# First product for V placed in column block 30 of peer_u, and the routing done by halves of the tokens and of the heads

## The chip, the cores and the metric

The kernel runs on one core of one Trainium2 chip. The metric is the device time of one execution in microseconds (us). The core has five engines, each with its own stream of instructions, in order: TensorE (PE: matmuls, and PEld for loading their stationary operand), VectorE (DVE), ScalarE (ACT), GpSimd (POOL) and SyncE (SP, which here only issues DMAs). They wait for one another through semaphores. DMA queues move data between device memory (HBM) and the on-chip memory (SBUF); matmuls write into 8 banks of PSUM.

## The reference

Two transformer blocks on 256 tokens of width 2048, all in float32. The change concerns the expert layer (PEER) of the first block. With 128 x 128 = 16384 experts, each token picks 16 experts for each of 8 heads by its scores against two sets of 128 sub-keys; the result is a sum over those experts:

```python
s = einsum('thpd,hpnd->thpn', q, sub_keys)          # token, head, half p, key n
s_half, i_half = top_k(s, 16)
cand = s_half[:, :, 0, :, None] + s_half[:, :, 1, None, :]       # 16 x 16 sums
top_s, pos = top_k(cand, 16)
idx = take_along_axis(cand_idx, pos)                # cand_idx = i0 * 128 + i1
g = softmax(top_s)
a = einsum('cd,ced->ce', x, expert_u[idx])
y = einsum('ce,ced->cd', g * gelu(a), expert_v[idx])
```

## The kernel before

**Dense instead of gathered.** The kernel doesn't gather rows of expert_u and expert_v. It multiplies all tokens with all of peer_u, takes gelu of all 256 x 16384 products, multiplies them with a matrix of gates that is zero except where a token picked an expert, and multiplies the result with all of peer_v. The gates lie in a scratch tensor in HBM, scr_g (16384 experts x 256 tokens), which is cleared earlier. The gelus lie in scr_a.

**Pieces.** Weights come in pieces of 128 x 1024 (512 KB). For each piece, in a fixed order, SyncE loads `raw` (NR = 5 buffers), ScalarE rounds it to `whi` (L1512), VectorE forms the rest `wlo` = raw - whi (L1746), and TensorE makes three products, whi and wlo with the high part and whi with the low part of the activations (L1322). whi and wlo have NH = 3 buffers each, so VectorE can be at most about two pieces ahead of TensorE. peer_u takes 256 pieces in 32 column blocks j of 8 pieces each; peer_v takes 256 pieces, 16 groups `sc` of 16. After each column block of peer_u, ScalarE takes gelu, TensorE transposes it, and SyncE stores it to scr_a (L2303).

**Routing.** It runs beside peer_u. For each half t of the tokens (128 of 256): 16 selections of the best 16 of 128 (`top16`, five instructions each, L1987 to L1995), the casts and sums of candidates (L2000, L2006), 8 selections of 16 of 256, the softmax (`gate_gap` L2013, `gate_exp` on ScalarE, `gate_norm` L2020 to L2024), the way back from places to keys (`rank_halves`, `rank_match`, `rank_pick`, `rank_sum`, L2032 to L2055) and `expert_ids` (L2061 to L2065).

**Scatters.** For every head and rank GpSimd issues one indirect DMA (`gate_scatter`, L2252) that adds 128 gates, one per token, to scr_g: 16 for a head, 128 for a half of the tokens, 256 in all. The first scatter of a head waits until the last of the head before it, of the same tokens, has landed. Behind the last one `fetch(sc)` brings the gelus (L2261) and the gates (L2262) of one group of experts back on chip. `prepare(sc)` multiplies the two on VectorE (`expert_gate`, L2079) and splits the product into its high part (ScalarE) and low part (`expert_split`, L2086). It consists of four parts with two products each, and peer_v's group sc reads it. `fetch` of group sc + 2 follows prepare(sc).

**What sets the order.** The program writes out all engines' instructions in one walk. Generators in two lists, `tasks` and `idle`, are advanced at each `step()`; the first of `idle` one step with (nearly) every piece. The routing is in `idle`, the scatters are in `tasks`, four per step. The walk knows nothing of time: "the scatters are done" means only that they are all written into GpSimd's stream. So with four scatters in a step, the program has written all 256 long before GpSimd can have run them. In the kernel before, the routing generator ends with both first fetches and `prepare(0)`, four steps after that.

Of the kernel before, what the change touches and what calls it, by code (L numbers as in the profile page):

```python
# [38 lines left out]
def build(nc, D, out):  # L39
# [12 lines left out]
    with ExitStack() as ctx:  # L52
# [134 lines left out]
        def walk(steps):  # L187
# [694 lines left out]
            def scatter():  # L882
                landed, rounds, t = [t_clear, t_clear], [0, 0], 1
                while len(g_written) < 2:
                    while not routed:
                        yield
                    if len(routed) == 2 and rounds[1 - t] < 8:
                        t = 1 - t
                    elif len(routed) == 1:
                        t = 0  # L890
                        if rounds[0] == 8:
                            yield
                            continue
                    h = rounds[t]
# [6 lines left out]
                    rounds[t] += 1  # L901
                    if rounds[t] == 8:
                        g_written.append(mark)

            def routing():
                tasks.append(scatter())
                for t in range(2):
                    for hp in range(16):
                        go("top16", SC[:, t, hp, :], V16[:, t, hp, :], I16u[:, t, hp, :], fresh("DVE", t_sc, everything))
                        last = up("DVE", "top16")  # L910
                        yield
                    go("i16_cast", t, fresh("DVE", last))
                    last = up("DVE", "i16_cast")
                    for h in range(8):
                        if h == 4:
                            yield
                        go("candidates", t, h, fresh("DVE", last))
                        last = up("DVE", "candidates")
                    yield
                    for h in range(8):  # L920
                        go("top16", cand[:, h].rearrange("p a b -> p (a b)"), W2[:, h, :], P2u[:, h, :], fresh("DVE", last))
                        last = up("DVE", "top16")
                        yield
                    sm, ri = stat(8), stat(8)
                    go("gate_gap", fresh("DVE", last))
                    a = up("DVE", "gate_gap")
                    go("gate_exp", fresh("ACT", a))
                    a = up("ACT", "gate_exp")
                    go("gate_norm", t, sm, ri, fresh("DVE", a))
                    tg = up("DVE", "gate_norm")  # L930
                    yield
                    go("rank_halves", fresh("DVE", last))
                    a = up("DVE", "rank_halves")
                    for q in range(2):
                        for h in (0, 4):
                            hs = slice(h, h + 4)
# [9 lines left out]
                    go("expert_ids", t, fresh("DVE", a))  # L946
                    routed.append([tg, up("DVE", "expert_ids")])
                    yield
                while len(g_written) < 2:
                    yield  # L950
                bar.append(everyone())
                fetch(0)
                fetch(1)
                for _ in range(4):
                    yield
                yield from prepare(0)
# [59 lines left out]
            for j in range(32):  # L1016
                pair, b, last = gemm("peer_u", 8 * j, 16, AH, AL, nA)
                u_post(pair, b, last, j)
                if j == 0:
# [3 lines left out]
                    idle.append(routing())  # L1023
            while len(wB.get(0, ())) < 4:
# [475 lines left out]
        def scalar_program(e):  # L1500
# [122 lines left out]
            def gate_exp(ready):  # L1623
# [811 lines left out]
```

## Time and profile before

| what | us |
|---|---|
| median of 3 timed runs | 3737.26 (3732.13 to 3737.8) |
| the profiled execution | 3733.21 |
| its span, first to last instruction | 3731.4 |
| TensorE busy | 3291.7 (88% of the span) |
| VectorE busy | 2052.6 (55%) |
| ScalarE busy | 1489.1 (40%) |
| GpSimd busy | 502.2 (13%) |

The profiler's page divides the span into 40 equal slices of 93 us and gives each engine's busy tenths, the granted TensorE clock in tenths of full speed, and the mean busy share of the DMA engines:

```profile
PE   7888999999000699999999999999999999999998
DVE  7666549874000344566666666555446555555556
POOL 2110000578777200000000000000000000000000
PEclk9989999999555899999999999999999999999999
DMA  4336556788222666677777765655465656666664
```

A time is read from the span's start. All views in this document come from this one execution. PE's busy time is modelled for pipelined matmuls, and an instruction's idle time is put down to the engine whose semaphore came last. The spans of GpSimd's instructions that issue a DMA show the issuing, not the transfer.

### The profile page before, as it was taken

What the parts mean: (1) busy time and instruction counts of PE and PEld (TensorE: products, weight loads), DVE (VectorE), ACT (ScalarE), POOL (GpSimd) and SP (SyncE); (2) the same over time, 40 slices, a digit from 0 to 9 for tenths busy, and PEclk for the clock granted to TensorE, in tenths of its full rate; (3) what the DMA queues carried; (4) which work ended last, traced back from release to release, by engine and by line L of the source; (5) the groups of instructions that cost most, each with busy time, mean ns of one, the idle gap of its engine ahead of it and who ended that gap; (6) DMA issues with size and microseconds to landing.
All of it is one profiled execution on the core that took longest, in us unless ns stands there. A gap on an engine that the chain in (4) does not pass through costs nothing.

```text
span 3731.4 us, 44636 instructions
## 1 busy us (share of the span) xinstructions
PE 3291.7 (88%) x18254; PEld 2867.0 (77%) x18254; DVE 2052.6 (55%) x2880; ACT 1489.1 (40%) x1883; POOL 502.2 (13%) x332
## 2 busy tenths in 40 slices
PE   7888999999000699999999999999999999999998
PEld 6667897878000588888888887898999799999996
DVE  7666549874000344566666666555446555555556
ACT  3345444444000344444444445444444454444443
POOL 2110000578777200000000000000000000000000
PEclk9989999999555899999999999999999999999999
DMA  4336556788222666677777765655465656666664
GB/s 156 114 110 229 170 176 198 207 203 209 12 0 0 197 209 208 200 245 248 249 239 239 237 193 167 186 152 164 147 181 181 197 159 189 188 187 187 186 191 152
DMA packets 214941, 659.07 MB, mean 177 GB/s; under 512 B 56097, under 2 KB 56097, under 8 KB 212177
## 3 DMA queue, kind: packets, MB, share of 16 engines
q1 hardware_dynamic: 165536, 598.74, 51.6%
q0 software_dynamic: 49200, 57.49, 7.4%
q8 instruction: 144, 2.36, 0.3%
q14 instruction: 61, 0.49, 0.0%
HBM read 620.35 MB, written 35.78 MB: 176 GB/s over the span
## 4 chain that ended last, share of the span: by engine, by line
PE 68%; POOL 11%; issue 4%; DVE 4%; DMA 2%; ACT 1%; DVEq 0%; ACTq 0%; POOLq 0%
PE bank L1322 67%; POOL scr_g L2252 11%; DMA scr_g<-M 2%; DVE wlo L1746 1%; PE bank L1364 1%; ACT whi L1512 0%; ACT M L1502 0%; DMA M<-scr_g 0%; DVE TMP L1809 0%; DVE R L2180 0%; DVE TMP L1810 0%; DVE M L1989 0%; ACT M L1554 0%; DVE M L1995 0%; DVE AL L1786 0%
## 5 line engine op out<-in xcount | busy, mean ns | idle before, releaser
L1746 DVE TENSOR_TENSOR wlo<-raw,whi 128x1024 fp32r<-128x1024 f32 x1101 | 1352.3, 1231 | 1126.0 <-ACT whi L1512 1121.8
L1512 ACT ACTIVATE whi<-raw 128x1024 fp32r<-128x1024 f32 x1101 | 1161.0, 1059 | 1371.0 <-PE bank L1322 1344.4
L1322 PE MATMUL bank<-whi,AH 128*128 128x512 f32 x1664 | 664.3, 399 | 319.0 <-DVE wlo L1746 318.8
L1322 PE MATMUL bank<-whi,AL 128*128 128x512 f32 x1664 | 653.1, 392 | 0.0
L1322 PE MATMUL bank<-wlo,AH 128*128 128x512 f32 x1664 | 652.6, 392 | 0.0
L1322 PE MATMUL bank<-whi,BH 128*128 128x512 f32 (+1 forms) x1608 | 626.1, 389 | 0.1
L1322 PE MATMUL bank<-wlo,BH 128*128 128x512 f32 (+1 forms) x1608 | 623.5, 388 | 0.0
L1322 PE MATMUL bank<-whi,BL 128*128 128x512 f32 (+1 forms) x1608 | 623.0, 387 | 0.0
L1322 PEld LDWEIGHTS bank<-whi,AH 128*128 128x128 f32 x1664 | 315.6, 190 | 387.6 <-DVE wlo L1746 316.8
L1322 PE MATMUL bank<-AH,whi 128*128 128x256 f32 (+1 forms) x2064 | 591.3, 286 | 0.3
L1322 PE MATMUL bank<-AH,wlo 128*128 128x256 f32 (+1 forms) x2064 | 583.9, 283 | 0.0
L1322 PE MATMUL bank<-AL,whi 128*128 128x256 f32 (+1 forms) x2064 | 583.8, 283 | 0.0
L2252 POOL DMA_INDIRECT scr_g<-M x256 | 430.8, 1683 | 479.0 <-issue 444.4
L1322 PEld LDWEIGHTS bank<-AH,whi 128*128 128x128 f32 (+1 forms) x2064 | 395.2, 191 | 2.1 <-DVE AL L1786 1.1
L1322 PEld LDWEIGHTS bank<-AL,whi 128*128 128x128 f32 (+1 forms) x2064 | 395.2, 191 | 0.9
L1322 PEld LDWEIGHTS bank<-AH,wlo 128*128 128x128 f32 (+1 forms) x2064 | 394.9, 191 | 0.1
L1322 PEld LDWEIGHTS bank<-whi,AL 128*128 128x128 f32 x1664 | 314.9, 189 | 68.0
L1322 PEld LDWEIGHTS bank<-wlo,AH 128*128 128x128 f32 x1664 | 315.7, 190 | 62.5
L1322 PEld LDWEIGHTS bank<-whi,BH 128*128 128x128 f32 x1608 | 302.7, 188 | 67.4 <-DVE wlo L1746 6.4
L1322 PEld LDWEIGHTS bank<-whi,BL 128*128 128x128 f32 x1608 | 302.8, 188 | 62.1
L1322 PEld LDWEIGHTS bank<-wlo,BH 128*128 128x128 f32 x1608 | 302.9, 188 | 60.6
L1502 ACT ACTIVATE BH<-M 128x512 fp32r<-128x512 f32 x96 | 60.2, 632 | 457.9 <-DVE M L2079 457.2
(238 smaller groups left out, 2012.4 us busy)
## 6 DMA issues: line engine op xcount, KB each, us to landing
raw<-in_peer_u SPq DMA_DIRECT2D x256, 512.0 KB
raw<-in_peer_v SPq DMA_DIRECT2D x256, 512.0 KB
raw<-in_w_in SPq DMA_DIRECT2D x160, 512.0 KB
raw<-in_w_up SPq DMA_DIRECT2D x128, 512.0 KB
raw<-in_w_down SPq DMA_DIRECT2D x128, 512.0 KB
raw<-in_w_out SPq DMA_DIRECT2D x64, 512.0 KB
raw<-in_w_in_a SPq DMA_DIRECT2D x32, 512.0 KB
scr_g<-M POOLq DMA_DIRECT2D x8, 2048.0 KB, 24.7
```

Source lines behind the costliest of these rows:

```text
L1322: return e.matmul(outp, l, r, start=start, stop=stop)
L1364: last = e.transpose(banks[bank][:, 128 * n:128 * n + 128], s, ident)
L1502: e.activation(o, x, func, **kw).then_inc(sem(name), 1)
L1512: e.activation(whi[:, n % NH, :], raw[:, n % NR, :], ACT.Copy).then_inc(s_hi, 1)
L1746: e.tensor_tensor(wlo[:, n % NH, :], raw[:, n % NR, :], bf(whi[:, n % NH, :]), ALU.subtract).then_inc(s_lo, 1)
L2252: e.indirect_dma_start(out=D["scr_g"].rearrange("e (t o) -> (e t) o", o=1), out_offset=bass.IndirectOffsetOnAxis(ap=EID[t][:, k:k + 1], ax ...
```

## The change

Three things are changed. The routing of each half of the tokens is done for heads 0 to 3 and then for heads 4 to 7, so that expert ids are ready in four portions instead of two; each portion's scatters may be issued as soon as it is ready. `gate_norm` stands behind the rank steps instead of ahead of them. And the first two fetches are written at column block j = 28 of peer_u, the first product `prepare(0)` after block 30, instead of right behind the routing. The step functions get the slice `hs` of four heads (expert_ids is shown, the others likewise); their instructions are the same on half as many columns. The line numbers of the kernel after are up to 2 higher or lower.

```diff
@@ -880,60 +880,57 @@
             def scatter():
-                landed, rounds, t = [t_clear, t_clear], [0, 0], 1
+                landed, rounds, n, t = [t_clear, t_clear], [[], []], 0, 1
                 while len(g_written) < 2:
-                    while not routed:
+                    while routed:
+                        half, ready = routed.pop(0)
+                        h0 = 4 * (n % 2)
+                        n += 1
+                        rounds[half] += [(h, ready) for h in range(h0, h0 + 4)]
+                    if rounds[1 - t]:
+                        t = 1 - t
+                    elif not rounds[t]:
                         yield
...
-                        go("gate_scatter", t, 16 * h + k, fresh("POOL", routed[t], landed[t] if k == 0 else None))
+                        go("gate_scatter", t, 16 * h + k, fresh("POOL", ready, landed[t] if k == 0 else None))
...
-                    if rounds[t] == 8:
+                    if h == 7:
                         g_written.append(mark)
...
             def routing():
                 tasks.append(scatter())
                 for t in range(2):
...
+                    for g in range(2):
+                        hs = slice(4 * g, 4 * g + 4)
+                        for hp in range(8 * g, 8 * g + 8):
+                            go("top16", SC[:, t, hp, :], V16[:, t, hp, :], I16u[:, t, hp, :], fresh("DVE", t_sc, everything))
+                            last = up("DVE", "top16")
+                            yield
+                        go("i16_cast", t, g, fresh("DVE", last))
...
+                        go("gate_gap", hs, fresh("DVE", last))
+                        a = up("DVE", "gate_gap")
+                        go("gate_exp", hs, fresh("ACT", a))
+                        te = up("ACT", "gate_exp")
+                        go("rank_halves", hs, fresh("DVE", last))
+                        a = up("DVE", "rank_halves")
                         yield
...
-                    go("expert_ids", t, fresh("DVE", a))
-                    routed.append([tg, up("DVE", "expert_ids")])
-                    yield
-                while len(g_written) < 2:
-                    yield
+                        go("gate_norm", t, hs, sm, ri, fresh("DVE", te))
+                        tg = up("DVE", "gate_norm")
+                        go("expert_ids", t, hs, fresh("DVE", a))
+                        routed.append((t, [tg, up("DVE", "expert_ids")]))
+                        yield
                 bar.append(everyone())
-                fetch(0)
-                fetch(1)
-                for _ in range(4):
-                    yield
-                yield from prepare(0)
...
@@ -1021,6 +1013,12 @@
                     sub_scores()
                     q_read = latest["PE"]
                     idle.append(routing())
+                if j == 28:
+                    assert not idle and len(g_written) == 2
+                    fetch(0)
+                    fetch(1)
+                if j == 30:
+                    idle.append(prepare(0))
...
+            def expert_ids(t, hs, ready):
+                for mark in ready:
+                    e.wait_ge(*mark)
+                s = slice(16 * hs.start, 16 * hs.stop)
+                a, b = idg[0][:, s], idg[1][:, s]
+                then(e.scalar_tensor_tensor(out=a, in0=a, scalar=128.0, in1=b, op0=ALU.mult, op1=ALU.add))
```

On **VectorE, at the first product for V**: before, the product (L2079, which waits for the fetch) stands behind 252 of the 1101 weight splits (L1746, of which x8 are eight in a row); L2070 is the copy of transposed gelus.

```order
L1746 TENSOR_TENSOR wlo<-raw,whi 128x1024 [waits hi_split] x8
L2070 COPY M<-bank 128x512 [waits gelu_stored0,transposed]
L1746 TENSOR_TENSOR wlo<-raw,whi 128x1024 [waits hi_split] x8
L2070 COPY M<-bank 128x512 [waits gelu_stored1,transposed]
L1746 TENSOR_TENSOR wlo<-raw,whi 128x1024 [waits hi_split] x8
L2070 COPY M<-bank 128x512 [waits gelu_stored0,transposed]
L2079 TENSOR_TENSOR M<-M 128x256 [waits gate_fetched0,gelu_fetched0]
L2079 TENSOR_TENSOR M<-M 128x256
L2086 TENSOR_TENSOR BL<-M,BH 128x512 [waits expert_hi]
L1746 TENSOR_TENSOR wlo<-raw,whi 128x1024 [waits hi_split]
L2079 TENSOR_TENSOR M<-M 128x256 x2
L2086 TENSOR_TENSOR BL<-M,BH 128x512 [waits expert_hi]
```

After, it stands (as L2081) behind 360 splits (here L1745):

```order
L2072 COPY M<-bank 128x512 [waits gelu_stored1,transposed]
L1745 TENSOR_TENSOR wlo<-raw,whi 128x1024 [waits hi_split] x8
L2072 COPY M<-bank 128x512 [waits gelu_stored0,transposed]
L1745 TENSOR_TENSOR wlo<-raw,whi 128x1024 [waits hi_split] x8
L2072 COPY M<-bank 128x512 [waits gelu_stored1,transposed]
L1745 TENSOR_TENSOR wlo<-raw,whi 128x1024 [waits hi_split] x4
L2081 TENSOR_TENSOR M<-M 128x256 [waits gate_fetched0,gelu_fetched0]
L2081 TENSOR_TENSOR M<-M 128x256
L2088 TENSOR_TENSOR BL<-M,BH 128x512 [waits expert_hi]
L1745 TENSOR_TENSOR wlo<-raw,whi 128x1024 [waits hi_split]
L2081 TENSOR_TENSOR M<-M 128x256 x2
L2088 TENSOR_TENSOR BL<-M,BH 128x512 [waits expert_hi]
```

The product has moved behind 108 further splits, which now run without waiting for the fetch.

On **VectorE, behind split 139**: before, the selections among the sums of candidates (L1987 to L1995) for the first half of the tokens.

```order
L1746 TENSOR_TENSOR wlo<-raw,whi 128x1024 [waits hi_split]
L2070 COPY M<-bank 128x512 [waits gelu_stored0,transposed]
L1987 MAX M<-M 128x8 [waits candidates]
L1989 MAX_INDEX M<-M 128x8 [waits vector_step]
L1991 MATCH_REPLACE M<-M 128x256 [waits vector_step]
L1993 MAX M<-M 128x8 [waits vector_step]
L1995 MAX_INDEX M<-M 128x8 [waits vector_step]
L1746 TENSOR_TENSOR wlo<-raw,whi 128x1024 [waits hi_split]
L1987 MAX M<-M 128x8 [waits top16]
```

After, behind the same number of splits, the end of the rank steps (L2049, L2055), the norm of the gates (L2019 to L2023) and the first expert ids (L2063 to L2067):

```order
L2049 TENSOR_TENSOR M<-M 128x1024 [waits rank_match]
L1745 TENSOR_TENSOR wlo<-raw,whi 128x1024 [waits hi_split]
L2055 TENSOR_REDUCE M<-M 128x64 [waits rank_pick]
L1745 TENSOR_TENSOR wlo<-raw,whi 128x1024 [waits hi_split]
L2019 TENSOR_REDUCE ST<-M 128x4 [waits gate_exp]
L2021 RECIPROCAL ST<-ST 128x4 [waits vector_step]
L2023 TENSOR_TENSOR M<-M,ST 128x64 [waits vector_step]
L2063 SCALAR_TENSOR_TENSOR M<-M 128x64 [waits rank_sum]
L2065 TENSOR_SCALAR M<-M,C 128x64 [waits vector_step]
L2067 CAST M<-M 128x64 [waits vector_step]
```

The first expert ids stand behind split 142; before they stood behind split 164 (all 128 columns). The later ones stand behind splits 166, 190 and 214; before, the second ones stood behind 210.

On **GpSimd, heads 3 to 5 of the first half of the tokens**: before, each row without a count is the first scatter of a head, waiting for the landing of the one before.

```order
L2252 DMA scr_g<-M 4194304x1 [waits gate_scattered0]
L2252 DMA scr_g<-M 4194304x1 x15
L2252 DMA scr_g<-M 4194304x1 [waits gate_scattered0]
L2252 DMA scr_g<-M 4194304x1 x15
L2252 DMA scr_g<-M 4194304x1 [waits gate_scattered0]
```

After, head 4 waits for its expert ids and gates too:

```order
L2254 DMA scr_g<-M 4194304x1 [waits gate_scattered0]
L2254 DMA scr_g<-M 4194304x1 x15
L2254 DMA scr_g<-M 4194304x1 [waits gate_scattered0,expert_ids,gate_norm]
L2254 DMA scr_g<-M 4194304x1 x15
L2254 DMA scr_g<-M 4194304x1 [waits gate_scattered0]
```

The order of the 256 scatters is the same in both kernels; only head 4 of either half of the tokens has a further wait.

## Rows read from the trace of the kernel before

**Rows 1.** Windows: stretch, busy us of each engine, granted PE clock, DMA share, GB/s.
```profile
681.00:939.00 258.00, 255.72 (x1164) 209.89 (x1162) 174.18 (x323) 111.19 (x124) 201.26 (x109) 1.00 0.84 206
939.00:1247.00 308.00, 0.00 (x0) 0.00 (x0) 2.70 (x5) 1.58 (x2) 232.54 (x152) 0.51 0.25 13
```

**Rows 2.** Waits of TensorE, 1247 to 1300 us: us in total, times, longest.
```profile
PE bank L1322 <- DVE wlo L1746: 308.2, 1, 308.2
```

**Rows 3.** TensorE in order of time: start us, us, line, operation, operands, idle before.
```profile
938.47 0.39 PE L1322 MATMUL bank<-whi,AL 128*128 128x512 f32 x1
1247.04 0.80 PE L1322 MATMUL bank<-whi,AH 128*128 128x512 f32 x1 [308.18 <-DVE wlo L1746]
```

**Rows 4.** VectorE in order of time, round the long wait.
```profile
932.54 0.68 DVE L2070 COPY M<-bank 128x512 f32<-128x512 f32 x1
1243.36 0.76 DVE L2079 TENSOR_TENSOR M<-M 128x256 f32<-128x256 f32 x2 [310.13 <-DMA M<-scr_g]
...
1245.76 1.23 DVE L1746 TENSOR_TENSOR wlo<-raw,whi 128x1024 fp32r<-128x1024 f32 x1 [0.25 <-ACT whi L1512]
```

**Rows 5.** GpSimd by time: first scatters of heads, the last, the fetch.
```profile
681.47 2.57 POOL L2252 DMA_INDIRECT scr_g<-M  x1 [358.46 <-issue]
...
724.72 2.33 POOL L2252 DMA_INDIRECT scr_g<-M  x1 [3.35 <-DMA scr_g<-M]
...
759.57 1.55 POOL L2252 DMA_INDIRECT scr_g<-M  x1 [2.12 <-DMA scr_g<-M]
...
796.15 1.55 POOL L2252 DMA_INDIRECT scr_g<-M  x1 [3.64 <-DMA scr_g<-M]
...
914.20 1.55 POOL L2252 DMA_INDIRECT scr_g<-M  x1 [4.21 <-DMA scr_g<-M]
...
980.29 1.55 POOL L2252 DMA_INDIRECT scr_g<-M  x1 [0.30 <-issue]
...
1011.44 1.55 POOL L2252 DMA_INDIRECT scr_g<-M  x1 [1.72 <-DMA scr_g<-M]
...
1231.29 1.55 POOL L2252 DMA_INDIRECT scr_g<-M  x1 [0.30 <-issue]
1234.89 0.60 POOL L2261 DMA_DIRECT2D M<-scr_a  x1 [2.05 <-DMA scr_g<-M]
1235.48 0.97 POOL L2262 DMA_DIRECT2D M<-scr_g  x1
```

**Rows 6.** SyncE by time: gelu stores, one a column block of peer_u.
```profile
586.48 0.33 SPq L2303 DMA_DIRECT2D scr_a<-M  x1
...
819.67 0.33 SPq L2303 DMA_DIRECT2D scr_a<-M  x1
...
933.30 0.33 SPq L2303 DMA_DIRECT2D scr_a<-M  x1
...
1266.19 0.33 SPq L2303 DMA_DIRECT2D scr_a<-M  x1
...
1288.91 0.33 SPq L2303 DMA_DIRECT2D scr_a<-M  x1
```

**Rows 7.** VectorE in order of time, round the first scatter.
```profile
595.96 1.23 DVE L1746 TENSOR_TENSOR wlo<-raw,whi 128x1024 fp32r<-128x1024 f32 x1 [1.03 <-ACT whi L1512]
...
678.03 1.23 DVE L1746 TENSOR_TENSOR wlo<-raw,whi 128x1024 fp32r<-128x1024 f32 x1 [0.84 <-ACT whi L1512]
...
680.41 0.23 DVE L2065 CAST M<-M 128x128 uint32<-128x128 f32 x1
```

**Rows 8.** Issue to landing of the fetches of scr_g, 1250 to 2200 us.
```profile
DMA to landing us min/median/max: 9.9/11.2/12.3
```

**Rows 9.** Scatter instructions: ns min/median/max, first and last start.
```profile
L2252 POOL DMA_INDIRECT scr_g<-M x256: 1552/1553/2607, 681.5 to 1231.3; - x128
```

**Rows 10.** Waits of TensorE while the routing runs, 530 to 935 us.
```profile
PE bank L1322 <- DVE wlo L1746: 4.0, 7, 1.1
PE bank L1364 <- ACT M L1502: 1.2, 1, 1.2
```

More of the change, by code:

```diff
@@ L907, in routing @@
                 for t in range(2):
-                    for hp in range(16):
-                        go("top16", SC[:, t, hp, :], V16[:, t, hp, :], I16u[:, t, hp, :], fresh("DVE", t_sc, everything))
-                        last = up("DVE", "top16")
+                    for g in range(2):
[5 more added lines that the diff above has]
+                        go("i16_cast", t, g, fresh("DVE", last))
+                        last = up("DVE", "i16_cast")
+                        for h in range(4 * g, 4 * g + 4):
+                            go("candidates", t, h, fresh("DVE", last))
+                            last = up("DVE", "candidates")
@@ L911, in routing @@
                         yield
[L912 to L915, printed above, removed]
+                        for h in range(4 * g, 4 * g + 4):
+                            go("top16", cand[:, h].rearrange("p a b -> p (a b)"), W2[:, h, :], P2u[:, h, :],
+                               fresh("DVE", last))
+                            last = up("DVE", "top16")
                             yield
-                        go("candidates", t, h, fresh("DVE", last))
-                        last = up("DVE", "candidates")
@@ L929, in routing @@
-                    go("gate_norm", t, sm, ri, fresh("DVE", a))
-                    tg = up("DVE", "gate_norm")
-                    yield
[L932 to L936, printed above, removed]
+                        sm, ri = stat(4), stat(4)
+                        go("gate_gap", hs, fresh("DVE", last))
+                        a = up("DVE", "gate_gap")
@@ L937, in routing @@
+                        go("gate_exp", hs, fresh("ACT", a))
+                        te = up("ACT", "gate_exp")
+                        go("rank_halves", hs, fresh("DVE", last))
+                        a = up("DVE", "rank_halves")
+                        yield
+                        for q in range(2):
                             go("rank_match", q, hs, fresh("DVE", a))
@@ L1621, in sub_out, with gate_exp @@
                 act(SC[:, t, h0:h0 + 4, :], banks[bank][:, :].rearrange("p (h n) -> p h n", h=4), ACT.Copy, "sub_out")
[L1623 removed]
+            def gate_exp(hs, ready):
                 for mark in ready:
                     e.wait_ge(*mark)
[L1626 removed]
+                w = idg[2][:, 16 * hs.start:16 * hs.stop]
+                act(w, w, ACT.Exp, "gate_exp")
             def gelu(ti, b, ready):
@@ L2056, in rank_sum @@
                                 ALU.add).then_inc(sem("rank_sum"), 1)
-            def expert_ids(t, ready):
+            def expert_ids(t, hs, ready):
                 for mark in ready:
                     e.wait_ge(*mark)
-                then(e.scalar_tensor_tensor(out=idg[0], in0=idg[0], scalar=128.0, in1=idg[1], op0=ALU.mult, op1=ALU.add))
+                s = slice(16 * hs.start, 16 * hs.stop)
+                a, b = idg[0][:, s], idg[1][:, s]
+                then(e.scalar_tensor_tensor(out=a, in0=a, scalar=128.0, in1=b, op0=ALU.mult, op1=ALU.add))
                 e.wait_ge(s_vec, at[0])
-                then(e.tensor_scalar(idg[0], idg[0], 256.0, token[:, t:t + 1], ALU.mult, ALU.add))
+                then(e.tensor_scalar(a, a, 256.0, token[:, t:t + 1], ALU.mult, ALU.add))
                 e.wait_ge(s_vec, at[0])
-                e.tensor_copy(EID[t], idg[0]).then_inc(sem("expert_ids"), 1)
+                e.tensor_copy(EID[t][:, s], a).then_inc(sem("expert_ids"), 1)
             def gelu_turned(gi, bank, ready):
```

52 lines of the change are left out of this document (17 added, 35 removed).

## The prediction

> **What bounds the kernel now.** I began with the page's slices: TensorE is busy for nine tenths or more almost everywhere, and not at all for some 300 us a quarter of the way in. The windows put numbers on it: from 681 to 939 us TensorE was busy for 255.7 of 258 us, from 939 to 1247 for none, and in that second stretch only GpSimd worked, 152 instructions [rows 1]. TensorE's waits name one wait of 308.2 us, for a split of weights on VectorE [rows 2]; in order of time it runs from 938.47 + 0.39 = 938.86 to 1247.04 [rows 3]. VectorE was not slow there, it stood at the first product for V: its last work ends at 932.54 + 0.68 = 933.2, and at 1243.36 it multiplies, after 310.13 us of waiting for the fetch of the gates [rows 4]. The fetch stands behind all 256 scatters on GpSimd: the first starts at 681.47, the last at 1231.29, the fetch is issued at 1234.89 and 1235.48 and lands 7.9 us later [rows 5]. So here the time is set by a series of scatters with a product queued too early in front of the weight splits, not by TensorE.
>
> What the stall costs in all is read where nothing else changes: SyncE stores once per column block of peer_u. In the steady state the stores lie 1288.91 - 1266.19 = 22.72 us apart (8 pieces, 2.84 us each), and the pair round the stall 332.89 us. The stall is worth 332.89 - 22.72 = **310.2 us**, 2.0 more than the wait itself [rows 6]. During that wait the granted clock was 0.51 on average [rows 1], that is, mostly the lower of the two levels, and the first matmul behind it took 0.80 us where the last one ahead took 0.39 [rows 3]; I put the 2.0 us down to that restart.
>
> **The place of the first product.** The change moves it on VectorE from behind 252 weight splits to behind 360, 108 pieces later, and moves the fetch with it in program order. The same instructions are issued, so nothing is removed; the 108 pieces that waited behind it now run ahead of it. Undisturbed, VectorE comes to it at 933.2 + 108 x 2.84 = 1240 us, and TensorE has splits in store until 938.86 + 306.8 = 1245.7 us. From VectorE's release to TensorE's restart it took 1247.04 - 1243.36 = 3.7 us [rows 3, 4]. TensorE therefore loses whatever the landing L of the first fetch lies past 1245.7 - 3.7 = 1242 us. What is late next is thus the same chain of scatters, and the question is whether it ends by 1242.
>
> **The chain of scatters, its start.** Halves of the heads are routed one by one. The first expert ids come behind split 142, where they came behind split 164. Split 164 began at 678.03 and the first scatter 3.4 us later [rows 5, 7]. Split 136 began at 595.96 [rows 7]; split 142 follows 6 x 2.84 = 17 us later at 613, with the gate's norm and the ids 3 us behind it: the first scatter starts at about 616, that is 65 us earlier. VectorE is near its limit there, which could make it 618. GpSimd does not run dry afterwards: later halves are ready every 24 pieces (68 us), while four heads of scatters take over 150 us.
>
> **Its pace.** The scatters remain one series, head by head, the first of each head waiting for the landing of the head before; the change doesn't interleave the two token halves, since in program order each half's heads are used up before the next is ready. So I price a head of 16 scatters with its wait. While VectorE also routes, three heads took 796.15 - 681.47 = 114.7 us, 38.2 each, the first of them 43.25 and the second 34.85. With the routing over and the products going on, three took 914.20 - 796.15 = 118.05, 39.35 each. With TensorE and VectorE idle a head took 1011.44 - 980.29 = 31.15 us [rows 5]. Most of the old series ran at that last pace; now TensorE and VectorE work throughout, so the slow paces hold. That gives back a part: the same event that is removed had let the scatters go fast. Routing ends behind split 214, about 616 + 72 x 2.84 = 820 us: 5.3 heads at 38.2 are 204 us, the other 10.7 at 39.35 are 420 us, and the series with its last landing is through at 616 + 204 + 420 = 1240 us. The fetch adds 0.6 us to its second issue [rows 5] and, beside the weight stream, 11.2 us to its landing (9.9 to 12.3) [rows 8]; L = 1251.5. **The residual stall is 1251.5 - 1242 = 9.5 us.** Its clock penalty I set at nothing, since the wait is short; its upper bound is the 2.0 us above.
>
> Where the slower pace comes from matters. A scatter instruction takes 1.55 us at the median but up to 2.61 [rows 9], and the long ones lie in the busy stretch: 2.57 and 2.33 at 681 and 724 us, 1.55 at all those in the quiet one [rows 5]. The Trainium skill (GPSIMD Engine Reference, 1. Specifications) says that GpSimd's way into SBUF is shared with VectorE, with contention when VectorE runs in a 2-port mode or reads two SBUF inputs. The weight split reads two. The rows agree in kind; by this rule the slow pace follows VectorE's work and so holds for every scatter now, which speaks against the full gain of this change. Were the pace in the quiet stretch the chain's own, 16 x 31.15 = 498 us from 616 would be over at 1114, and the residual would be zero; that is the second case below.
>
> **Small parts.** The routing is cut finer: cast, gap, norm, halves and ids are issued four times for 4 heads instead of twice for 8. An id step took 0.23 us for 128 columns [rows 7]; with a bound of 0.3 us each, the 24 additional instructions are at most 7 us of VectorE, spread over 94 pieces, and less because they are half as wide. ScalarE gets four exponentials rather than two, each between gelus, behind a wait for VectorE; weight splits queue behind that wait. In the old routing TensorE waited 4.0 us for VectorE and 1.2 for ScalarE [rows 10], and ten column blocks took 819.67 - 586.48 = 233.2 instead of 227.2 us, 6.0 too long [rows 6]. The new routing spreads the four long selections of each half between lighter steps, and VectorE does not wait for ScalarE's exponential, since the norm stands behind the rank steps. Bounds: all 6.0 gone, or 6.0 more through two more exponentials. I take -2. The products for the first two groups now stand 8 pieces apart near the end of peer_u instead of far apart. A product, its own split and one weight split took VectorE from 1243.36 to 1245.76 + 1.23, 3.6 us [rows 4], 0.8 over the pace of a piece, and there are four; the 1245.7 - 1240 = 5.7 us of splits in store hide these 3.2 us, and if a stall has used them up they cost at most 3.2.
>
> **Sum.** The profiled execution took 3733.2 us. 3733.2 - 310.2 + 9.5 - 2 = 3430.5. The three timed runs before were 3732.1 to 3737.8, their median 4.1 above the profiled one; I add about half of that and forecast **3432 us**.
>
> **Rivals.** *The scatters end in time.* If heads take (1242 - 12 - 616) / 16 = 38.4 us or less on average, nothing is left: 3733 - 310 - 2 = 3421, and 3417 if the routing costs nothing; 3414 with the lowest of the timed runs and some slack. For: the second head, in full load, took 34.85, and 16 of those end at 1174. Against, though narrowly: the mean of all six loaded heads is 38.8, that of the last three 39.35.
> *The scatters are slower for longer.* At 41.3 us a head, L = 616 + 661 + 12 = 1289 and 47 us are left: 3468. At the slowest, 43.25, L = 1320, residual 78: about 3501. For: DMA engines were busy to 0.84 beside the scatters [rows 1], for 258 us; now this lasts 600. Against: only one loaded head was so slow, and it lay beside the routing.
> *Slower than before, by a collapse of the scatters under load.* The mechanism: with scatters, weights and gelu stores together, landings of single elements queue, and each head waits on the one before. It decides where L passes 1242 + 310 = 1552, which needs (1552 - 616 - 12) / 16 = 57.8 us a head, 1.34 times the slowest head seen. Price at 60 us: L = 1588, 36 us slower than before, 3769. Nothing in the trace is near that.
> *The change doesn't reach the wait.* Excluded for the place: the instruction order shows 108 splits moved ahead. What doesn't happen is an overlap of landings between the token halves, and I count none.
>
> **How the numbers follow.** Residual of 1 to 27 us (3422 to 3450), heads of 38.5 to 40.1 us: 0.50, with 3432 as its number. None: 0.33. More than 27 us but far from the old time: 0.14. Gain lost altogether or almost: 0.01 within 0.2% (which is what a measurement of this kernel can tell from no change), 0.02 slower. The range goes from 3414, none left and a cheap routing, to 3468, the third case down to 41.3 us a head; beyond it lie some 1 in 10.
>
> **What would show it.** Right: the first scatter near 616; heads of 38 to 40 us all the way, the long instructions no longer ending at 933 us; column blocks 22.72 us apart to block 30; then one wait of VectorE for the fetch near 1240, with a shorter one of TensorE for a split, about 10 us. The stores after that stand some 300 us earlier than before. Wrong at the start: a first scatter past 620, or gaps in which GpSimd waits for expert ids. Wrong at the pace: heads of 31 us although VectorE works (then the shared way is not the cause), or over 41. Wrong at the price: many small waits of TensorE in peer_u for weights or splits, which would mean that the scatters take from the weight stream.

## The result, and the profile after

The changed kernel takes 3449.3 us, the median of 4 runs (3442.9 to 3452.6), against 3737.3; the ratio is 0.923, with a 95% interval of 0.9213 to 0.9247. The forecast was 3432, the range 3414 to 3468. The profiled execution took 3452.6 us (span 3450.8), the slowest of the four, where that of before took 3733.2: 280.6 us less. The slices of the page (now 86 us each):

```profile
PE   7878999999999979999999999999999899999998
...
DVE  6766546887444436666666665554455555555555
...
POOL 1100000677787840000000000000000000000000
PEclk9989999999999989999999999999999999999999
DMA  4417565778888877777776555554566566666664
```

The gap of zeros has gone from TensorE's row; behind the first few slices one 7 is left (the fifteenth), at the place the product for V now has. GpSimd is busy from slice 8 to 15 with the scatters, and VectorE beside it all the way. TensorE's waits between 530 and 1400 us (in all, times, longest) answer to [rows 2, 10]:

```profile
PE bank L1320 <- DVE wlo L1745: 26.7, 13, 22.2
PE bank L1362 <- ACT M L1500: 1.2, 1, 1.2
```

One wait of 22.2 us stands where 308.2 stood. VectorE's side of it answers to [rows 4]:

```profile
1240.57 1.22 DVE L1745 TENSOR_TENSOR wlo<-raw,whi 128x1024 fp32r<-128x1024 f32 x1 [2.40 <-ACT whi L1510]
1265.55 0.76 DVE L2081 TENSOR_TENSOR M<-M 128x256 f32<-128x256 f32 x2 [23.76 <-DMA M<-scr_g]
```

VectorE is through with its last split at 1240.57 + 1.22 = 1241.8 us and waits for the fetch until 1265.55. TensorE restarts at 1269.24, and its first matmul takes 0.79 us as in [rows 3], which is the slow level again:

```profile
1269.24 0.79 PE L1320 MATMUL bank<-whi,AH 128*128 128x512 f32 x1 [22.17 <-DVE wlo L1745]
```

GpSimd's first scatter, the first one of the sixth head, the last one and the fetch answer to [rows 5]:

```profile
617.66 2.21 POOL L2254 DMA_INDIRECT scr_g<-M  x1 [294.69 <-issue]
...
817.90 2.08 POOL L2254 DMA_INDIRECT scr_g<-M  x1 [3.59 <-DMA scr_g<-M]
...
1253.31 1.55 POOL L2254 DMA_INDIRECT scr_g<-M  x1 [0.30 <-issue]
1256.97 0.60 POOL L2263 DMA_DIRECT2D M<-scr_a  x1 [2.10 <-DMA scr_g<-M]
1257.56 0.97 POOL L2264 DMA_DIRECT2D M<-scr_g  x1
```

The stores of gelu, one for each column block, answer to [rows 6]:

```profile
588.02 0.33 SPq L2305 DMA_DIRECT2D scr_a<-M  x1
...
821.50 0.33 SPq L2305 DMA_DIRECT2D scr_a<-M  x1
...
1230.19 0.33 SPq L2305 DMA_DIRECT2D scr_a<-M  x1
...
1280.48 0.33 SPq L2305 DMA_DIRECT2D scr_a<-M  x1
...
1306.28 0.33 SPq L2305 DMA_DIRECT2D scr_a<-M  x1
```

The blocks between the first two are ten. The two blocks round the product took 1306.28 - 1230.19 = 76.1 us. The same two blocks before (the last of peer_u, where no product had to wait):

```profile
1538.90 0.33 SPq L2303 DMA_DIRECT2D scr_a<-M  x1
...
1590.42 0.56 SPq L2303 DMA_DIRECT2D scr_a<-M  x1
```

They took 1590.42 - 1538.90 = 51.5 us (and 52.1 us in the interleaved kernel further down, which has the product there and no stall). So the residual stall cost 76.1 - 51.5 = 24.6 us in all: 22.2 of waiting and 2.4 behind it. The granted clock over that place (the windows' columns are those of [rows 1]):

```profile
1230.00:1281.00 51.00, 28.83 (x122) 23.50 (x121) 16.66 (x23) 13.53 (x17) 23.13 (x17) 0.77 0.66 179
```

It was 0.77 on average, so part of the stretch ran at the lower level. Even a wait of 22 us brings the clock down for a moment. How long, the matmuls behind the wait show; this is the first at the old pace again:

```profile
1274.00 0.40 PE L1320 MATMUL bank<-whi,AL 128*128 128x512 f32 x1
```

From 1269.24 up to it there are eleven, 4.8 us; ahead of the wait eleven took 11 x 0.227 = 2.5 us (30 in a row from 1239.67 to 1246.47). That is 2.3 us, and agrees with the 2.4.

### The profile page after: what moved, and what is told of

The parts are those of the page before. It is cut to its first block, busy times and chain, and to the rows that moved or that the text cites. A ratio compares the mean times of both kernels' runs of the same rounds, so it can differ in the third digit from the quotient of the medians.

```text
span 3450.8 us, 44667 instructions
## 1 busy us (share of the span) xinstructions
PE 3296.2 (96%) x18254; PEld 2870.4 (83%) x18254; DVE 2054.1 (60%) x2904; ACT 1493.9 (43%) x1889; POOL 567.7 (16%) x332
## 4 chain that ended last, share of the span: by engine, by line
PE 79%; DVE 6%; ACT 2%; issue 1%; DMA 0%; POOL 0%; DVEq 0%; ACTq 0%; POOLq 0%
PE bank L1320 78%; DVE wlo L1745 2%; PE bank L1362 1%; ACT whi L1510 1%; ACT M L1500 0%; DVE M L1988 0%; DVE M L1994 0%; DVE M L1992 0%; DVE M L1990 0%; DVE M L1986 0%; DMA M<-scr_g 0%; POOL scr_g L2254 0%; DVE M L2005 0%; DVE TMP L1808 0%; DVE TMP L1809 0%
## 5 line engine op out<-in xcount | busy, mean ns | idle before, releaser
L1745 DVE TENSOR_TENSOR wlo<-raw,whi 128x1024 fp32r<-128x1024 f32 x1101 | 1352.2, 1231 | 1129.1 <-ACT whi L1510 1124.4
L2254 POOL DMA_INDIRECT scr_g<-M x256 | 496.4, 1939 | 435.5 <-issue 385.5
```

The source lines that it names most:

```text
L1745: e.tensor_tensor(wlo[:, n % NH, :], raw[:, n % NR, :], bf(whi[:, n % NH, :]), ALU.subtract).then_inc(s_lo, 1)
L2254: e.indirect_dma_start(out=D["scr_g"].rearrange("e (t o) -> (e t) o", o=1), out_offset=bass.IndirectOffsetOnAxis(ap=EID[t][:, k:k + 1], ax ...
```

## The experiments

The theory after the result: the place of the product removes the whole of the old stall; what is left is the distance between VectorE's arrival at the product (1242 us) and the landing of the fetch behind the scatters; and the scatters' pace of 40 us a head is set by VectorE's work and by the weight transfers together. Rivals were named with each experiment. "A head" is always 16 scatters with the wait for a landing ahead of the next; the mean over a kernel is (issue of the fetch - first scatter) / 16.

**One part of the change alone: the place.** The routing is that of before; only the first product and the fetch are moved.

```diff
                 while len(g_written) < 2:
                     yield
                 bar.append(everyone())
-                fetch(0)
-                fetch(1)
-                for _ in range(4):
-                    yield
-                yield from prepare(0)
...
+                if j == 28:
+                    assert not idle and len(g_written) == 2
+                    fetch(0)
+                    fetch(1)
+                if j == 30:
+                    idle.append(prepare(0))
```

> The routing as in the kernel before, by halves of the tokens alone; only the first two fetches and the first product for V stand where the change puts them (behind 360 weight splits instead of 252). My theory: the place alone removes the old stall of 310 us, and the late start of the scatters, 681 us instead of 618, comes back one for one at the new place. Scatters at 40 us a head end at 681 + 640 = 1321, the fetch lands at 1330, TensorE waits until 1334 where it could have gone on at 1247: a wait of about 87 us, median about 3737 - 310 + 89 = 3516. Rival: the place does it all and the routing by quarters adds nothing (median within 5 us of the changed kernel, 3449).

Measured: 3492.1 us (3490.5 to 3493.4, 4 runs), ratio 0.9346 (0.933 to 0.9361). TensorE's wait:

```profile
PE bank L1323 <- DVE wlo L1747: 67.5, 9, 63.2
```

The rival falls: with this place alone 43 us of the change's gain are missing. But the wait is 63 us and not 87. The scatters began at 684.2 and the fetch was issued at 1299.4: heads of 38.45 us, not 40. The last two took 32.5 and 34.4 us, since TensorE and VectorE stood by then; that is 13 of the 25 us that the series was faster than I had counted. The other 12 are the fourteen heads ahead of them, 39.2 us each where I had taken 40. **A stall that waits for the scatters also speeds them up**, so it did not grow one for one with their lateness; I had used this for the old kernel and forgotten it here.

**The other part alone: the routing by quarters.** Fetch and product stand right behind the written scatters again.

```diff
+                while len(g_written) < 2:
+                    yield
                 bar.append(everyone())
+                fetch(0)
+                fetch(1)
+                for _ in range(4):
+                    yield
+                yield from prepare(0)
...
-                if j == 28:
-                    assert not idle and len(g_written) == 2
-                    fetch(0)
-                    fetch(1)
-                if j == 30:
-                    idle.append(prepare(0))
```

> The routing by quarters as in the change, but fetch and first product stand right behind the written scatters, as in the kernel before; since these are written earlier, the product comes behind 238 splits. My theory: the scatters start at 618 as in the changed kernel, but VectorE stops at about 893, 40 us earlier than before, so that 144 scatters run while all else is idle: they end near 1184, and TensorE waits about 297 us from 899 on. The routing alone is worth next to nothing: median about 3725. Rival: the 64 us of earlier start come out in full, 3673.

Measured: 3717.4 us (3715.0 to 3722.1, 4 runs), ratio 0.9951 (0.9935 to 0.9968).

```profile
PE bank L1321 <- DVE wlo L1746: 295.1, 13, 290.5
```

Forecast were 297 us of waiting and 3725; it is 290.5 and 3717. An earlier start of the scatters is worth 20 us where the product stands too early, and 3492 - 3449 = 43 us where it stands late: the parts are not additive, because the place decides what is beside the scatters. Here the product stands behind 238 splits instead of 252, so VectorE stops some 40 us sooner, and the last eight heads run beside nothing, seven of them at 31 to 33 us.

**The place moved on: 364 and 367 splits.** The scatters are those of the change.

```diff
+            def waited():
+                for _ in range(4):
+                    yield
+                yield from prepare(0)
...
                 if j == 30:
-                    idle.append(prepare(0))
+                    idle.append(waited())
```

> The changed kernel with the first product behind 364 splits: half the way. VectorE comes to it at 1253, the fetch lands at about 1267; VectorE waits 14 us, TensorE 11 to 12. Median about 3439. If the time does not fall in steps of about 11 us over the places 360, 364 and 367, the stall is not what sets the time here.

Measured: 3441.8 us (3439.1 to 3445.2, 4 runs), ratio 0.9215 (0.9201 to 0.9229).

```profile
PE bank L1325 <- DVE wlo L1750: 18.4, 16, 12.1
```

```diff
-                if j == 30:
+                if j == 31:
                     idle.append(prepare(0))
```

> The changed kernel, scatters as they are, with the first product behind 367 splits instead of 360: VectorE comes to it 7 x 2.84 = 20 us later, at about 1262, the fetch lands at 1266 to 1270. The wait of TensorE falls from 22 to 0 to 6 us, median 3427 to 3435. Rival: the products, now directly ahead of the pieces of peer_v that need them, bring a new wait of 10 us or more, and the median stays above 3440.

Measured: 3437.0 us (3435.9 to 3438.2, 4 runs), ratio 0.92 (0.9186 to 0.9214).

```profile
PE bank L1320 <- DVE wlo L1745: 7.2, 16, 1.2
PE bank L1320 <- DVE BL L2088: 3.7, 1, 3.7
```

The wait for a split falls with the place as it should, 22.2, 12.1, and then no long one. But the medians go 3449, 3442, 3437: by 7 and 5 us, not by the 11 each that I had named as the sign that the stall alone sets the time; the last lies 2 us past its forecast range. So a later place has a price of its own. In the last one TensorE waits 3.7 us for BL, the product itself, which is now directly ahead of the pieces of peer_v that read it: a wait as the rival said, but not of 10 us. The rest of the price is measured further down, where the same step is made without a stall (7.8 us); 22 us of waiting less 7.8 and 3.7 leaves 10.5, near the 12.3 between the medians.

**Another order of the routing: the token halves alternate.** The order of the four portions changes, and two scatters instead of four are written per step, so that the portions are there in time to alternate. Now the landing of a head is covered by a head of the other token half. No run takes the two edits apart.

```diff
-                        h0 = 4 * (n % 2)
+                        h0 = 4 * (n // 2)
...
-                        if k % 4 == 3:
+                        if k % 2 == 1:
                             yield
...
-                for t in range(2):
-                    for g in range(2):
+                for g in range(2):
+                    for t in range(2):
```

> The changed kernel with the four portions routed in another order (heads 0 to 3 of both token halves, then heads 4 to 7 of both), and two scatters written per step instead of four. From the fourth head on the heads of the two token halves alternate for the most part, so that the landing a head waits for is usually one head old. My theory: the 14 waits for a landing (49.7 us in the changed kernel) shrink to 3 or 4, the heads take 36 to 37.5 us in place of 40, the series is through by about 1215, VectorE finds the fetch landed when it comes to the product at 1241, and the residual wait of 22 us goes: median about 3449 - 25 = 3424. Rival: the landings were hiding other waits (GpSimd's queue, the transfers themselves), heads stay at 39 to 40 us, median 3445 to 3450.

Measured: **3424.0 us** (3422.9 to 3425.4, 5 runs), ratio 0.9163 (0.9151 to 0.9176), faster than both kernels of the case. GpSimd's idle time for a landing (us, times), and TensorE's waits from 530 to 1400 us:

```profile
  DMA scr_g<-M: 13.5, 4
```

```profile
PE bank L1320 <- DVE wlo L1745: 4.9, 13, 0.5
PE bank L1362 <- ACT M L1500: 1.2, 1, 1.2
```

The landing waits went from 49.7 us in 14 to 13.5 us in 4, the heads from 39.96 to 37.3 us, the fetch was issued at 1214.8, before VectorE came to the product, and the wait of 22.2 us is gone. What is left of TensorE's waits is that of the old routing [rows 10]. The first fetch stood 42 us earlier than in the changed kernel, and only the 24.6 us of the stall came out as time: 3449.3 - 3424.0 = 25.3. The rest is slack now.

The same with the product at the later place:

> As the interleaved one, with the first product written behind column block 31 instead of 30 (behind 367 splits instead of 360). Where no stall is left, a later place gives nothing: within 3 us of the interleaved kernel, about 3424. Rival: the products for the first two groups, now back to back at the start of peer_v, keep TensorE waiting for 5 to 10 us.

Measured: 3431.8 us (3429.3 to 3432.8, 4 runs), ratio 0.9186 (0.9172 to 0.92). My forecast (no difference) was wrong and the rival right, with 7.8 us. Over the 93 us round the end of peer_u (1227 to 1320, and 1230 to 1323 in the interleaved kernel, which is 3 us later there) TensorE is busy for 87.4 us instead of 92.7, in small waits. Where nothing is late, the later place only crowds the products of the first two groups in front of peer_v.

**What makes a head take 40 us: without VectorE's splits.** The low part of peer_u's weights is left out of the result: ScalarE writes zeros.

```diff
+                if order[n][0] == "peer_u":
+                    e.activation(whi[:, n % NH, :], raw[:, n % NR, :], ACT.Copy)
+                    e.activation(wlo[:, n % NH, :], raw[:, n % NR, :], ACT.Copy, scale=0.0).then_inc(s_hi, 1)
+                    return
...
+                if order[n][0] == "peer_u":
+                    e.tensor_copy(wlo[:, n % NH, 0:1], bf(wlo[:, n % NH, 0:1])).then_inc(s_lo, 1)
+                    return
```

> The changed kernel with the low part of peer_u's weights left out: ScalarE writes zeros to wlo in an activation beside the one for whi, and VectorE only copies one column of it to pass the semaphore on. The transfers and the matmuls are as many as before; VectorE's split with two SBUF inputs is gone from peer_u. If the slow pace of the scatters comes from VectorE (the shared way into SBUF): heads of 31 to 33 us once the routing is over, no scatter instruction above 1.7 us there, the series through by 1170, no stall at the product. If it comes from the weight transfers or from TensorE: heads stay at 39 to 41 us and the wait of about 22 us stays.

Measured: 3413.2 us (3412.9 and 3413.5), ratio 0.9133 (0.9115 to 0.9152). The scatter instructions (ns min/median/max, first and last start) and the idle time for landings, in the changed kernel and then in this one:

```profile
L2254 POOL DMA_INDIRECT scr_g<-M x256: 1551/1670/2566, 617.7 to 1253.3; - x128
...
  DMA scr_g<-M: 49.7, 14
```

```profile
L2261 POOL DMA_INDIRECT scr_g<-M x256: 1551/1552/2025, 612.6 to 1164.1; - x128
...
  DMA scr_g<-M: 55.2, 14
```

The stretch in which TensorE and the transfers work as before and VectorE hardly does (busy 22 of 270 us, DMA share 0.83):

```profile
860.00:1130.00 270.00, 270.00 (x1238) 223.41 (x1237) 22.01 (x107) 206.70 (x227) 195.24 (x126) 1.00 0.83 207
```

The long instructions are gone: a median of 1.55 us, and in the second half of the series each head's mean is 1.55 where the changed kernel's is 1.94. A head takes 34.8 us (35.1 once the routing is over), not 31 to 33: 3.6 us over the pace of the quiet stretch [rows 5] are left, and the waits for landings are at least as long as in the changed kernel (55.2 us in 14). So VectorE is the larger cause, and something else is another; the next run asks whether it is the transfers. TensorE has no waits for VectorE at all between 530 and 1400 us here, which gives 9 us beside the stall: ten blocks of the routing take 227.3 us instead of 233.5, and the ones ahead of them 2.6 less.

**Without the transfers.** Seven eighths of each later piece of peer_u are not loaded; the products use what lay there.

```diff
+                if name == "peer_u" and k >= 8:
+                    e.dma_start(raw[:, m % NR, 0:128], D[name][k, :, 0:128]).then_inc(s_raw[m % NR], 16)
+                    return
```

> The changed kernel with peer_u's pieces from the ninth on loaded to an eighth (128 of 1024 columns); the rest of a piece keeps what lay in the buffer, so the products differ. The splits on ScalarE and VectorE and the matmuls are as many and as long as before; only the transfers beside the scatters are gone. A head takes 31.2 us with all idle, 40.0 with both, and 34.8 with the transfers but without VectorE's splits. If the two causes add up, VectorE's part is 5.2 us and the transfers' 3.6: heads of 36 to 37 us, scatter instructions as long as in the changed kernel (1.95 us on average), the waits for landings down from 3.6 to below 2 us each, the series through at about 1205, no wait at the product, time about 3425. Rival: the transfers also lengthen the instructions, which then take 1.55 to 1.7 us, heads 32 to 34 us.

Measured: 3423.8 us (3423.5 and 3424.1), ratio 0.9165 (0.9138 to 0.9191).

```profile
L2254 POOL DMA_INDIRECT scr_g<-M x256: 1552/1575/2567, 615.7 to 1217.1; - x128
...
  DMA scr_g<-M: 30.0, 14
```

```profile
860.00:1180.00 320.00, 320.00 (x1468) 264.77 (x1467) 146.03 (x127) 140.53 (x156) 250.75 (x130) 1.00 0.83 208
```

```profile
860.00:1180.00 320.00, 320.00 (x1468) 264.76 (x1467) 146.57 (x127) 139.36 (x155) 261.73 (x137) 1.00 0.35 47
```

The last two rows are the same 320 us in the changed kernel and in this one: TensorE, VectorE and ScalarE are equally busy, the transfers fell from 208 to 47 GB/s (a DMA share of 0.35 is left of 0.83). The waits for landings fell from 3.6 to 2.1 us each. The instructions stayed long (1.91 us on average against 1.94), as forecast and against the rival. A head took 37.8 us; forecast were 36 to 37, so the transfers gave less back than the 3.6 I had put to them. Four cases stand side by side now, us per head: nothing beside the scatters 31.2 (single heads of the old stall), transfers 34.8, VectorE 37.8, both 40.0 (means over a whole series). VectorE's part is 40.0 - 34.8 = 5.2 to 37.8 - 31.2 = 6.6 us, that of the transfers 2.2 to 3.6. TensorE and ScalarE work in the last three cases and stand in the first, and no run takes away VectorE's splits and the transfers while they work; so the upper bounds may hold up to 1.4 us that belong to them.

**VectorE's splits doubled.**

```diff
+                if order[n][0] == "peer_u" and order[n][1] >= 106:
+                    then(e.tensor_tensor(wlo[:, n % NH, :], raw[:, n % NR, :], bf(whi[:, n % NH, :]), ALU.subtract))
+                    e.wait_ge(s_vec, at[0])
```

> The changed kernel with VectorE's weight split done twice for the pieces of peer_u behind the routing; the same transfers and matmuls. VectorE is busy for 2.5 of each piece's 2.84 us, so TensorE is still fed. If VectorE's work makes the scatters slow, the excess over the quiet pace doubles: 40 - 31 = 9 becomes up to 18, heads of 45 to 49 us, and the wait at the product grows from 22 to some 80 to 110 us. If the transfers make them slow: heads of 39 to 41 us and the wait unchanged.

Measured: 3459.0 us (3458.6 and 3459.3), ratio 0.9256 (0.9237 to 0.9274). TensorE's longest wait is 22.8 us, a head takes 39.9: neither grew. (The profiled execution is 6.0 us longer than that of the changed kernel. By the stores, 2.1 of it lie ahead of the first doubled split, 1.3 in the block where the doubling begins, and 3.2 in the last two blocks.) By my own words this was to mean that the transfers make the scatters slow; the kernel without splits says that for the most part they do not. The two agree only if the form of my theory falls: the delay does not follow the share of time in which VectorE is busy. What does it follow? In the changed kernel, two scatters and the splits beside them:

```profile
1018.07 2.42 POOL L2254 DMA_INDIRECT scr_g<-M  x1 [0.30 <-issue]
...
1023.51 1.55 POOL L2254 DMA_INDIRECT scr_g<-M  x1 [0.30 <-issue]
```

```profile
1017.83 1.23 DVE L1745 TENSOR_TENSOR wlo<-raw,whi 128x1024 fp32r<-128x1024 f32 x1 [1.49 <-ACT whi L1510]
...
1023.75 1.22 DVE L1745 TENSOR_TENSOR wlo<-raw,whi 128x1024 fp32r<-128x1024 f32 x1 [1.97 <-ACT whi L1510]
```

The first split runs from 1017.83 to 1019.06; the scatter of 1018.07 starts inside it and ends at 1020.49, 1.43 us behind the split's end. The scatter of 1023.51 starts 0.24 us ahead of the next split shown and takes the plain 1.55 us, with the split running beside most of it. In the kernel with doubled splits:

```profile
1020.79 2.09 POOL L2257 DMA_INDIRECT scr_g<-M  x1 [0.30 <-issue]
```

```profile
1020.24 1.22 DVE L1746 TENSOR_TENSOR wlo<-raw,whi 128x1024 fp32r<-128x1024 f32 x1
1021.49 1.22 DVE L1748 TENSOR_TENSOR wlo<-raw,whi 128x1024 fp32r<-128x1024 f32 x1
```

The scatter starts inside the first of two splits, which ends at 1021.46, and ends itself at 1022.88, again 1.42 behind it, although the second split runs from 1021.49 on. So a scatter waits at its start for the one VectorE instruction that is running, and not for the next. This holds beyond these three. In the changed kernel 118 scatters of the 256 start inside a split with more than 0.23 us of it to go (an end 1.42 us behind it is then later than 1.65 us, and can be told from the plain 1.55): 117 of them end 1.41 to 1.45 us behind the split's end, and no scatter that starts outside every VectorE instruction takes over 1.65 us.

It also explains why doubling changed so little. A scatter held by the first split of a pair ends 1.42 us behind it, when the second (1.22 us) is over too, and the next scatter, 0.30 us later, meets the first split of the next pair, where without doubling it meets the next split. From 860 to 1225 us 92 of 144 scatters took over 1.7 us with the doubled splits and 73 of 146 without, but the mean went only from 1.95 to 1.99 us.

Is it any VectorE instruction, or one of a kind? The routing of the changed kernel has both kinds, of equal length, and the scatters beside them start at the same point of each:

```profile
674.09 1.97 POOL L2254 DMA_INDIRECT scr_g<-M  x1 [0.30 <-issue]
...
676.36 1.55 POOL L2254 DMA_INDIRECT scr_g<-M  x1 [0.30 <-issue]
```

```profile
673.41 1.22 DVE L2049 TENSOR_TENSOR M<-M 128x1024 f32<-128x1024 f32 x1
...
675.68 1.21 DVE L2055 TENSOR_REDUCE M<-M 128x64 f32<-128x1024 f32 x1
```

Both scatters start 0.68 us into the instruction. The one beside `rank_pick` (L2049, which multiplies two operands in SBUF) ends 1.43 us behind it; the one beside `rank_sum` (L2055, which reads a single one) takes the plain 1.55 us and ends 1.02 behind it. All nine scatters that start well inside `rank_match` or `rank_pick` are held in this kernel, and none of the four inside `rank_sum`; over the traces of all eleven kernels it is 98 of 98 and none of 51. The Trainium skill (GPSIMD Engine Reference, 1. Specifications) says that GpSimd shares its way into SBUF with VectorE and names contention with instructions that read two SBUF inputs; these rows agree, and taking such instructions away from peer_u took the delay away.

## Why the prediction was right, and where it was off

**The stall.** Right: its 310.2 us are gone, and its cause was the place (the place alone gives 245 of the 288 us). This term carries the forecast; the residual stall, forecast at 9.5 us, came out at 24.6, and the paragraphs below say by which terms.

**VectorE's arrival.** 1240 was forecast, 1241.8 measured.

**The start of the scatters.** 616 forecast, 617.7 measured. The rule that GpSimd would not run dry held.

**Their pace.** This term was mis-sized. Forecast: 38.2 us a head beside the routing and 39.35 after it, 39.0 on average; measured 39.96. Beside the routing, five heads took 817.90 - 617.66 = 200.2 us, 40.0 each, one of them 46.7; after it, eleven took 1256.97 - 817.90 = 439.1, 39.9 each. I had three heads of each kind, and among the first three one of 34.85 and one of 43.25: too few for a term that is multiplied by 16. The two kernels that differ only in the product's place have the same scatters and took 40.0 (364 splits) and 39.6 (367), so the pace is no accident of one execution, though the head of 46.7 is in part (47.6 and 41.2 there). The series ended at 1257.0 instead of 1240, 15 us of it by the pace. (The landing L also was added up a little short: 1240 + 0.6 + 11.2 is 1251.8, not 1251.5.)

**The landing of the fetch.** Forecast 11.2 us from the issue of scr_g, measured 1265.55 - 1257.56 = 8.0, about as in the old stall (7.9): TensorE and the weight stream had stopped again (0 GB/s from 1247 to 1257 us). This gave back 3 us.

**From the landing to the loss.** The relation (landing less 1242) gives 23.5 us for the landing at 1265.55; TensorE waited 22.2. The clock penalty I had put at nothing "since the wait is short" is 2.4 us, a little over the upper bound of 2.0 that I had named: the short wait cost no less than the long one.

**The routing.** Forecast -2, measured about +2: ten blocks took 821.50 - 588.02 = 233.5 us (before 233.2), and the first of them begins 1.5 us later than before. The waits of TensorE there did not fall (4.5 us for splits in 12 waits besides the long one, 1.2 for ScalarE). In the kernel without VectorE's splits these 6 us are gone: they come from the load that routing and splits together put on VectorE, which the finer cut leaves as it was.

**The rest.** 3733.2 - 310.2 + 24.6 + 1.8 = 3449.4; the profiled execution took 3.2 more. These are found after the expert layer, at the same work, in the clock (200 us each, of before and of after):

```profile
2514.45:2714.45 200.00, 191.72 (x1357) 180.33 (x1356) 104.18 (x150) 86.22 (x121) 3.23 (x6) 0.99 0.51 156
```

```profile
2230.06:2430.06 200.00, 191.71 (x1334) 179.66 (x1333) 102.79 (x148) 84.64 (x119) 3.22 (x6) 0.97 0.50 153
```

The granted clock is 0.97 instead of 0.99 there; TensorE is as long busy, but for 23 matmuls fewer, which is some 3 us. It seems to be of this execution, not of the change: the other three runs lie 1 to 10 us lower, and of the traces of the other kernels, whose work is the same there, only that with the doubled splits loses about as much. No run shows why.

**The rivals.** That the scatters end in time became true only with the alternating order (and where splits or loads are left out), and then the time, 3424.0, is 3 us over the 3421 worked out for it. The slower pace of 41.3 us was not reached. The rule on the shared way was rightly taken as a reason for the slow pace; the quiet pace would have promised 3421 for the change. But it does not make the delay follow VectorE's busy time, as the doubled splits show. A collapse under load did not show; the longest time from one scatter's start to the next was 8.5 us.

## What to carry to other kernels

Where one program order is written for all engines, "done" in the writing is not done in time: work out when a slow series (here 256 scatters at 2.5 us) ends, count how many steps of the waiting engine lie ahead of that, and put the first instruction that needs it just behind. Price the series at the pace that it has beside the work, not at the pace within the stall that you remove, take that pace from as many rows as there are, and expect it to speed up again in any new stall. Placed late enough, nothing is gained by later still: in the interleaved kernel the last 20 us of delay cost 8.

## What the runs showed of the hardware

A GpSimd instruction that issues an indirect DMA took 1.55 us alone. When it started while a VectorE tensor_tensor of two SBUF operands was running (1.22 us), it ended 1.41 to 1.45 us behind that instruction's end, and so took up to 2.57 us. A reduction of one operand of the same length did not hold it, nor did a second tensor_tensor that began after it; and the splits that began beside it took their plain 1.22 to 1.23 us. Waits for the landing of 16 indirect DMAs were 3.6 us beside a stream of 208 GB/s and 2.1 beside 47. A TensorE wait of 22 us cost 2.4 us of time at the lower clock behind it, one of 308 us 2.0 (by the matmuls themselves 2.3 and 1.5).
